# The first block's two attentions: two stages with a barrier between them, or one pipeline of 48 row blocks

## What is computed

```
proj = rms_norm(h) @ w_in -> qa ka va qi ki wi qb kb vb gate_a gate_b
# index: score every earlier token, keep the best 128 of them per query
iscore = sum_h relu(qi_h . ki) * wi_h, causal;  sel = top_k(iscore, 128)
# attention A: 8 query heads of 64, one key/value head, softmax over sel only
o_a = softmax(qa . ka / 8, over sel) @ va
# attention B: 4 heads, each the difference of two causal softmax maps
o_b = (softmax(q1 . k1 / 8) - lam * softmax(q2 . k2 / 8)) @ vb     # vb is 128 wide
o_b = rms_norm(o_b, g_subln) * (1 - lam_init)
mix = sigmoid(gate_a) * (o_a @ w_branch_a) + sigmoid(gate_b) * (o_b @ w_branch_b)
h = h + mix @ w_out
```

## Time and profile before

| | |
|---|---|
| median of three runs | 3479.12 us (3471.82 to 3483.51) |
| the profiled execution | 3473.41 us, its span 3471.6 us |
| PE busy | 3182.2 us, 92% of the span |
| POOL, DVE, ACT busy | 45%, 48%, 41% |
| DMA | mean 76 GB/s, q1 in use for 24.6% of the span |

### The profile page before, as it was taken

How to read it: one execution, slowest core, us unless ns; L and a number is a source line. 1 busy time by engine, 2 the same in 40 slices (tenths; PEclk the granted TensorE clock), 3 DMA queues, 4 the chain that set the end, 5 groups by cost and what they waited for, 6 DMA issues and landing times. The chain is left out here.

```text
span 3471.6 us, 39165 instructions
## 1 busy us (share of the span) xinstructions
PE 3182.2 (92%) x14620; PEld 2475.1 (71%) x14620; DVE 1679.7 (48%) x2524; ACT 1434.4 (41%) x2281; POOL 1576.5 (45%) x870
## 2 busy tenths in 40 slices
PE   7978999999998799999999968899999985979999
PEld 6655688878776567887878736578877862758887
DVE  2673347731358533775245884433313785443320
ACT  4826533333384564333343444432223354352221
POOL 4623545544564355554555332344445432234443
PEclk8989999999899999999999978999999997889999
DMA  3211233333221122333322101123333200213333
GB/s 113 61 55 42 68 93 97 97 97 103 76 61 61 35 62 93 98 97 95 108 82 90 50 12 44 61 85 97 98 96 98 68 25 20 72 48 98 96 98 103
DMA packets 73740, 265.09 MB, mean 76 GB/s; under 512 B 8656, under 2 KB 9168, under 8 KB 73168
## 3 DMA queue, kind: packets, MB, share of 16 engines
q1 hardware_dynamic: 73552, 262.59, 24.6%
HBM read 260.46 MB, written 2.10 MB: 76 GB/s over the span
## 5 line engine op out<-in xcount | busy, mean ns | idle before, releaser
L365 POOL TENSOR_TENSOR low<-raw,high 128x1024 fp32r<-128x1024 f32 x482 | 1171.1, 2432 | 1289.2 <-ACT high L356 1269.3
L380 PE MATMUL bank<-slot_r,low 128*128 128x512 f32 (+2 forms) x3636 | 1434.5, 395 | 0.0
L381 PE MATMUL bank<-slot_r,high 128*128 128x512 f32 (+2 forms) x3636 | 1431.9, 394 | 0.0
L379 PE MATMUL bank<-slot_r,high 128*128 128x512 f32 (+1 forms) x3316 | 1337.6, 403 | 75.0 <-POOL low L365 30.8
L356 ACT ACTIVATE high<-raw 128x1024 fp32r<-128x1024 f32 x482 | 506.7, 1054 | 821.3 <-PE bank L381 761.0
L379 PEld LDWEIGHTS bank<-slot_r,high 128*128 128x128 f32 x3316 | 635.0, 192 | 260.1 <-issue 69.6
L380 PEld LDWEIGHTS bank<-slot_r,low 128*128 128x128 f32 (+1 forms) x3636 | 696.6, 192 | 149.0 <-issue 9.4
L381 PEld LDWEIGHTS bank<-slot_r,high 128*128 128x128 f32 (+1 forms) x3636 | 695.5, 191 | 149.4
L1583 DVE SCALAR_TENSOR_TENSOR tmp<-padded,small,tmp 128x512 f32<-128x512 f32 x176 | 210.0, 1251 | 0.0
L840 POOL TENSOR_SCALAR tmp<-tmp,stat 128x512 f32<-128x512 f32 (+3 forms) x128 | 71.5, 559 | 193.0 <-DVE stat L815 169.2
L509 ACT ACTIVATE slot_r<-slots,small 128x512 fp32r<-128x512 f32 (+1 forms) x80 | 54.7, 683 | 207.8 <-DVE slots L1591 73.4
(11 more groups left out here) (310 smaller groups left out, 3584.1 us busy)
## 6 DMA issues: line engine op xcount, KB each, us to landing
raw<-w SPq DMA_DIRECT2D x482, 512.0 KB, 3.6
slots<-x_in SPq DMA_DIRECT2D x4, 512.0 KB, 6.6
slots<-mem_in SPq DMA_DIRECT2D x2, 1024.0 KB, 5.0
out<-slots SPq DMA_DIRECT2D x8, 256.0 KB, 4.8
const<-const_in SPq DMA_DIRECT2D x1, 1073.5 KB, 10.8
padded<-p_in SPq DMA_DIRECT2D x2, 512.0 KB, 5.5
tmp<-masks_in SPq DMA_DIRECT2D x1, 512.0 KB, 11.5
small<-small SPq DMA_DIRECT2D x2, 231.5 KB, 2.7
```

What stands on the lines that cost most here:

```text
L365: pool.tensor_tensor(self.low[:, t % PARTS, :], self.raw[:, t % RING, :], self.high[:, t % PARTS, :].bitcast(F32), ALU.subtract).then_inc( ...
L379: pe.matmul(acc, lhs[0], rhs[1], start=first, stop=False)
L380: pe.matmul(acc, lhs[1], rhs[0], start=False, stop=False)
L381: return pe.matmul(acc, lhs[0], rhs[0], start=False, stop=last)
```

## The change

The two attention stages become one, with 48 units: B's 16 and then A's 32. `attention_work` takes several kinds of heads; a table lists for each unit its kind, head and row block, `first[n]` is the number of maps before unit n. The column of a statistic becomes its number modulo 32. The scores of A's first units are made in the steps in which B's last units are turned. There is no barrier between them.

B's norms go to other steps: heads 0 and 1 are squared at step 11 and summed at steps 12 and 14, heads 2 and 3 are squared at step 19 and summed at 20 and 22. Ln and Exp follow one step later on ACT, DVE scales two steps after the sum, ACT makes the high part three steps after it and POOL the low part at unit sum + 4. The buffers and the arithmetic stay.

A gate tile moves into the projection: after the last value tile PE multiplies it into bank 2, and DVE evacuates it after the selection (`EARLY = 22`). Then nine gate tiles are in B's steps 0 to 16 as before and six (before: seven) in halves at steps 26 to 48. In the loop of the projection all steps do 3 rounds of selection, the stage ends after 39, and the 9 others are in steps 4 to 12.

```
-    GATE = (40, 41, 42, 43, 44, 45, 46, 47, 52, 24, 25, 26, 56, 53, 54, 55)
+    GATE = (40, 41, 42, 43, 44, 45, 46, 47, 52, 53, 24, 25, 26, 56, 54, 55)
-    EARLY, WITH_B, SELECTED = 21, 9, 38
+    EARLY, WITH_B, SELECTED = 22, 9, 39
 # first_project, PE, behind the four value tiles
+                pe.wait_ge(sem("sin_done"), NR)
+                dense(pe, weights, banks[2][:, :], u_all)
 # ACT, behind the copies of B's values
+                weights.split_high(act, base + EARLY + 2)
 # DVE
-                        selection.rounds(2 if j < 11 else 3, (j - FIRST_IDX - 1) // 2)
+                        selection.rounds(3, (j - FIRST_IDX - 1) // 2)
                 selection.rounds(SELECTED - selection.done)
+                dve.wait_ge(sem("tile_done"), base + EARLY)
+                dve.tensor_tensor(S[:, GATE[0], :], banks[2][:, :], rs[:, :], ALU.mult)...
 # attention_work, POOL, a unit of A
+                    if n >= 1 and units[n - 1][0]["maps"] == 2:
+                        pool.wait_ge(sem("prob_ready"), n)
 # first_attentions
+        UB, N = 4 * NT, 12 * NT
+        n_gates = 2 * KC - 1
+        first_late = N - 4 * (n_gates - WITH_B) + 2
+        OB_SUM = {12: 0, 14: 1, 20: 2, 22: 3}
+        halves = {(2 * n, place): (n, half) for n in range(WITH_B) for half, place in enumerate(("scores", "turns"))}
+        halves.update({(first_late + 4 * (n - WITH_B) + 2 * half, "scores"): (n, half) for n in range(WITH_B, n_gates) for half in range(2)})
+        scaled_at = {min(step + 1, N): n for (step, _), (n, half) in halves.items() if half}
 # PE
+            if (step, place) in halves:
+                gate_half(pe, weights, *halves[step, place], tile)
+            if place == "turns" and step in OB_SUM:
+                h = OB_SUM[step]
+                pe.wait_ge(sem("ob_square"), h + 1)
+                if h >= 1:
+                    pe.wait_ge(sem("ob_log"), h)
+                pe.matmul(banks[6][:, :], cst("ones"), low[h], ...)
+            if place == "values" and step > 2 * NT + 2:
+                pe.wait_ge(sem("ob_log"), 2 if step == UB + 2 else 4)
 # ACT
+            if step in (UB // 2 + 3, UB + 3):
+                for h in ((0, 1) if step < UB else (2, 3)):
+                    act.wait_ge(sem("out_ready"), h + 1)
+                    act.activation(low[h], S[:, OB + h, :], ACT.Square)...
+            if step - 1 in OB_SUM:        # Ln, Exp
+            if step - 3 in OB_SUM:        # high part
 # DVE, at the end of a step
+            if step in scaled_at:
+                gate_scale(dve, base, scaled_at[step], GATE[scaled_at[step] + 1])
+            if 4 <= step < UB:
+                selection[0].rounds(1 if step < UB - 1 else selection[0].total)
+            if step - 2 in OB_SUM:
+                dve.wait_ge(sem("ob_rstd"), h + 1)
+                dve.scalar_tensor_tensor(x, x, col[:, SUB_GAIN:SUB_GAIN + 1], high[h], ALU.mult, ALU.mult)...
```

More of the change, by code:

```diff
@@ new lines, in attention_work @@
+    def attention_work(*kinds, side_act=None, side_dve=None, side_pool=None, side_pe=None):
+        units, first, heads = [], [0], []
+        for a in kinds:
+            for two in range(0, a["heads"], 2):
+                for r in range(2 * NT):
+                    units.append((a, two + r % 2, len(heads) + r % 2, r // 2))
+                    first.append(first[-1] + a["maps"])
+                heads += [a, a]
+        N = len(units)
+        owner = [n for n in range(N) for _ in range(units[n][0]["maps"])]
+        double = [sum(units[j][0]["maps"] == 2 for j in range(n)) for n in range(N + 1)]
+        biased = kinds[0]["bias"] is not None
@@ L684, in attention_work, with width @@
         E, LOGIT = 0, 4
[L685 removed]
+        lag, PROB = (2, (8, 9)) if biased else (4, (4, 5, 6, 7))
         depth = len(PROB)
+        def width(n):
+            return units[n][0]["width"](units[n][3])
         def prob(n):
[L690 to L695 removed]
+            return tmp[:, PROB[n % depth], 0:width(n)]
@@ L697, in run_pe, with st, half_of @@
+        def st(row, s, n=1):
+            return stat[:, row, s % 32:s % 32 + n]
+        def half_of(a, g):
+            b = (64 * (g % 2)) if a["m_out"] == 64 else 0
+            return b, b + a["m_out"]
         def run_pe(pe):
             def scores(n):
-                h, i = unit(n)
-                for m in range(maps):
-                    s = n * maps + m
+                a, h, g, i = units[n]
+                for m in range(a["maps"]):
+                    s = first[n] + m
                     if s >= 4:
-                        pe.wait_ge(sem("max_ready" if bias else "exp_done"), s - 3)
-                    pe.matmul(banks[s % 4][:, 0:width(i)], q(h, m, i), k(h, m, width(i)), start=True,
+                        pe.wait_ge(sem("max_ready" if biased else "exp_done"), s - 3)
+                    pe.matmul(banks[s % 4][:, 0:width(n)], a["q"](h, m, i), a["k"](h, m, width(n)), start=True,
@@ L1234, in side_dve @@
                 selection.append(Selection(dve, sem, selbias, top8, lambda i: S[:, SELECT + i, :], done=SELECTED))
-            if place == "end":
-                if step % 2 and step // 2 < WITH_B:
-                    gate_scale(dve, base, step // 2, GATE[step // 2])
-                if step >= 2:
-                    selection[0].rounds(1)
-                if step == 4 * 2 * NT // 2:
-                    gate_scale(dve, base, WITH_B - 1, GATE[WITH_B - 1])
-                    selection[0].rounds(selection[0].total)
@@ L2336, in second_tail @@
         K_SQ, K_R = PT[:, 0, 0, :], PT[:, 0, 1, :]
-        work = attention_work(
+        work = attention_work(one(
             4, 1, 0.125, lambda h, m, i: S[64 * (h % 2):64 * (h % 2) + 64, XQ + h // 2, i * P:i * P + P],
```

237 lines of the change are left out of this document (98 added, 139 removed).

## The result

| | before | changed |
|---|---|---|
| median (runs, spread) | 3478.00 us (8, 3471.14 to 3483.51) | 3456.88 us (8, 3452.67 to 3467.43) |
| profiled execution, its span | 3473.41, 3471.6 us | 3452.67, 3450.7 us |
| PE, DVE, ACT, POOL busy | 92%, 48%, 41%, 45% | 92%, 49%, 42%, 46% |
| mean granted clock | 0.951 | 0.954 |

The ratio is 0.9948, with a 95% interval of 0.9938 to 0.9959: 0.52% or 18 us faster by the comparison, 21 by the medians, where 26 were forecast.

What follows compares the result with a forecast made beforehand. PE was taken as the bound, with gains only before A's step 12 and, behind it, only from removing PE work. Terms of -14.1 and -11.7 us a layer made -25.8, giving 3453 us; 8 in 10 range 3437 to 3471.

Steps and rivals of the forecast that it cites:

- Start of B: Projection's end: DVE ends earlier with fewer late selection rounds, so B starts 1.5 us earlier per layer.
- B's first gate at the higher clock: B's first gate tile: PE stands 3.1 us, not 10.1, so less low clock; -0.7 us, bounds 0 and -2.3.
- Rounds out of steps 2 and 3: Selection in B: step 4's second-turn join comes one round earlier, its 2.47 us wait falls to 1.0; -1.5 us.
- B's last steps: Scores of step 12 to B's second values: norms of heads 0 and 1 and A's first scores add 4.3 us.
- Drain, barrier, fill: B's second values to step 28: 26.5 us instead of 41.2; -14.7 us in layer 0, -12.3 in layer 1.
- To the tail: From step 28 to the tail: eleven half gates at eleven steps as before, 56.6 us, unchanged.
- The sum: All terms together: -14.1 us in layer 0 and -11.7 in layer 1, -25.8 us in total.
- the first: Rival: ACT's Ln and Exp under B reach PE's path, 16 us back, 3469 us; chance 0.13.
- the second: Rival: gate-free steps 18 to 25 run at lower clock, +5 us a layer at half speed, 3463; chance 0.10.
- the fourth: Rival: DVE's in-order wait for Exp (steps 14, 16, 22, 24) costs 6.0 us a head, 3501; chance 0.05.
- the fifth: Rival: the projection's gate tile delays the barrier, taking back up to 2 x 5.5 us, 3464; chance 0.04.
- the third: Rival: more comes free in join waits, B's first gate and the fill, 15 us more, 3438; chance 0.12.

Runs made afterwards that it cites:

- merge only: Changed kernel without the gate tile in the projection and with the selection as before, seven late gates from step 22: 3470.00 us, ratio 0.9986.
- no Ln and Exp: Changed kernel with plain copies in place of Ln and Exp for B's heads 0 and 1, no table loads there: 3454.32 us, one run.
- changed again: The changed kernel repeated with no edit, for a second trace: 3455.95 us, ratio 0.9943.
- old selection: Changed kernel, merge and gate tile kept, with selection rounds placed as before (38 in the projection, ten in B's steps 2 to 11): 3464.11 us, ratio 0.9969.
- more rounds: Changed kernel with a fourth selection round at j = 12 and 15 of the projection's loop: 3453.53 us, ratio 0.9924.
- gate only: Kernel before, two stages and barrier kept, with only the gate tile moved into the projection: 3472.16 us, ratio 0.9993.
- two gates: Changed kernel with a second gate tile in the projection and five late gates in halves from step 30: 3453.69 us, ratio 0.9924.
- scaling later: Changed kernel with DVE's scaling of B's heads, ACT's high part and POOL's low part one step later each: 3467.23 us, one run.

## Why the prediction was right, and where it was not

The time was right in its direction and nearly in its size. By its own steps, per layer:

- *Start of B, -1.5: failed in this execution.* +0.8. DVE's list was counted right in instructions (B starts at 31.56 where L574 wins its race), but moving the rounds put L574 under a split of POOL: +2.5. The prediction asked for every moved instruction what it costs, and not what it meets. Over the ten layers with the same instructions B starts 32.7 after V in the mean, a gain of 0.3.
- *B's first gate at the higher clock, -0.7: not there.* The first 10 us of B have a clock of 0.75 (0.72 before), PE having stood 5.47 us and not the 3.1 forecast. Nor did a stand near 3.1 bring it: behind 2.9 to 3.4 us the clock was 0.68 to 0.83 in other traces. It was 1.00 only in three layers, behind 1.6 to 1.8 us.
- *Rounds out of steps 2 and 3, -1.5: the wait right, the sum of the stretch partly luck.* The wait of step 4 went from 2.47 to 0.84, as forecast. A growth of 1.15 in a gate's evacuation was missed. From B's start to the first values it is -3.8, where these two terms make -2.2; from 10 us behind B's start on the clock is 1.00 and was 0.93. The mean of the ten layers, 58.5, makes it -2.2 as well, so what goes beyond belongs to this execution.
- *B's last steps, +4.3: right,* 4.4, but not by the terms forecast: without the selection's move it is 3.8 ("merge only"), and the round in step 12, put at 0, costs the other 0.6. The waits for the joins of units 13 and 15 grew from 1.01 to 1.55 and from 0.51 to 0.97, the one for unit 17 is 0.81. Both joins run beside a split of POOL, as they did before. (The join that the prediction says ends together with its split ends 0.3 us behind it, at 220.07 against 219.78.) B's scalings, which the prediction feared under a split, met none: 0.74 or 0.75 us each in all eight. Ln and Exp cost nothing, as "no Ln and Exp" shows, and the ACT block of a head is 4.0 us: loads of 1.28 at 268.65 and 270.65, Exp ending at 272.59, with nothing between the four instructions here either.
- *Drain, barrier, fill, -14.7 and -12.3: right,* -15.6 and -13.2. 25.6 us where 26.5 was forecast. The prediction's own pieces don't make its 26.0: 13.8 to the end of Exp, then 3.2, 1.4 and 8.5 are 26.9. Measured they are 13.25, 2.3, 1.55 and 8.5. Nor is there the 0.5 for the low clock: with a clock of 0.93 or of 1.00 in this stretch it takes 25.56 to 25.60, in all ten layers that have these instructions (changed, changed again, old selection, more rounds, no Ln and Exp; five of each clock). The half gates cover waits: the two that "merge only" has more than "old selection" cost it 3.4 us of 5.5.
- *To the tail, 0: right,* 56.5.
- *The sum:* the errors of the terms, +2.3, +0.7, -2.3, +0.1, -0.9, cancel to -0.1. This is luck in its last digit: the second execution of the same kernel has another set of terms and a sum of -26.8.
- *From the sum to the time:* -25.9 in the stretches is -18 to -21 in time. 3.2 us of the difference are seen. The first 10 us of the tail, before and changed, both layer 1 (layer 0 is alike in both kernels):

```profile
1278.68:1288.68 10.00, 10.00 (x44) 8.28 (x45) 5.39 (x5) 7.50 (x12) 6.31 (x4) 1.00 0.36 107
```
```profile
1251.89:1261.89 10.00, 10.00 (x37) 8.09 (x38) 4.09 (x3) 7.48 (x12) 6.16 (x3) 0.83 0.35 107
```

Seven matmuls fewer, 1.6 us at 0.23, in each layer. The clock is 1.00 in all four tails of the kernel before, in both of "gate only" and in one of "old selection"; it is 0.83 or 0.84 in all other merged tails. The 10 us ahead of it are the same instructions in the same time, with the same wait of 2.27 (2.33 in layer 1) at the barrier. Why the merged kernels draw the lower clock there stays open.

The rest stays open too, and it doesn't look like scatter alone. Take the medians of one set of runs, less 1.9 us that lie outside of the span and less each kernel's own stretches. Before and "gate only" leave 3028 and 3029 us; "changed again", "merge only" and "old selection" leave 3036, 3038 and 3040. So the three merged kernels seem to lose 8 us or more outside of the changed stretches, of which the tail's clock is 3.2 at most. In the later sets the merged kernels with one gate leave 5 to 6 more than before, those with two gates no more than before. The stretches are those of one execution each, so this is an indication; where the other microseconds lie no trace here shows.

Of the rivals, the first is rejected by "no Ln and Exp", the second by the 25.6 us, which are the same at a clock of 0.93 and 1.00 (its mechanism does appear with two gates, where the values ran at half the clock), the fourth by the sum of the stretches and by "scaling later" (1.2 us a layer to be had, not 6 a head), the fifth by the tile that is done at 28.27 after V, with DVE at 32.84. Of the third, the waits on joins did not go; the fill lost more than forecast.

## What to carry to other kernels

Merging the two stages gave back 12.2 and 9.9 us a layer of drain, barrier and fill, for 3.8 us that went into the first stage. A piece of filler work is worth its own length only where nothing waits under it: the gate tile of 5.5 us gave 1.7 us a layer in the two-stage kernel and 3.9 in the merged one, or 0.7 and 2.8 without the stretch in B whose length changes from execution to execution. The half gate in step 26 shows the other side: without it the wait stayed and the clock fell, and the stretch became 2.3 us longer. When work is moved on an engine, walk the engine it shares a port with as well: an instruction of 0.36 us that lands under a 2.4 us one ate the gain at B's start. Compare the stretches that the change touches, cut at the same instructions, and repeat the kernel before as a control, before a difference of 10 us in 3470 is believed or explained.

## What the runs showed of the hardware that was not expected

- A single-input `TENSOR_SCALAR` of 128x384 floats took 0.36 us alone and 2.43 to 2.60 us behind a split on POOL; who started first, by as little as 0.02 us, decided which of the two was late. It went one way in five of ten layers with the same instructions and the other way in the other five, once both ways in one execution.
- Two executions of one kernel differ by 11 us in stretches with the same instructions, in steps, where the granted clock is lower for a few tens of us; the changed stretches of the same two agree to 0.2 us in the sum.
- Sixteen matmuls of values took 2.37 us at a clock of 1.00, and 4.54 at 0.50 behind waits of 3.61 and 1.11 us; with 12 matmuls of filler in place of the 3.61 it was 1.00.
- The clock at a stage's start after a wait of 2.27 us at a barrier was either 1.00 or 0.83, with the same 10 us ahead of it; 1.6 us of PE's work hang on it.
